# A hybrid decoder layer on one core: sums of weight blocks formed in the rounds of the FFNs and kept in HBM, and three orders changed

## Chip, core and metric

The kernel runs on 1 core of a Trainium2 chip, in one launch. The metric is the device time of that core in microseconds. Before the change it is 2225.57 us, the median of three runs (2220.57, 2225.57, 2229.49).

## What is computed

One layer on x of 1024 tokens x 1024 features, all in float32:

```python
h = swiglu(rmsnorm(x), w_gate, w_up, w_down)      # (silu(x@w_gate) * (x@w_up)) @ w_down, D_FF = 2816
x = x + 0.5 * rmsnorm(h)
h = hybrid_mixer(rmsnorm(x), ...)                 # one projection; dilated attention beside a Mamba-2 scan; w_out
x = x + rmsnorm(h)
h = swiglu(rmsnorm(x), ...)                       # second FFN, other weights
x = x + 0.5 * rmsnorm(h)
```

The change touches the two FFNs and the passage from the first FFN to the projection of queries, keys and values.

## The kernel before

**Split operands.** Every product of two float32 matrices is made of three matmuls on a high and a low part: w_hi x_hi, w_hi x_lo, w_lo x_hi. ScalarE rounds a raw tile to its high part (`*_hi`), VectorE subtracts (`*_lo`). TensorE can start when both are there.

**The FFN's rounds.** The 2816 inner features are 22 tiles of 128. The first two are computed plainly (`plain`, four units of a tile and half of the tokens: gate scaled, up scaled, SiLU on ScalarE, product, on VectorE L823 to L829). The other 20 run in pairs, i = 1 to 10 with s = 0, 1, each as seven block products of 12 matmuls (`seven_pe`) instead of eight: sums and differences of quarter blocks go in, and VectorE adds the results up (`tile` in `ffn_dve`). In the same tile VectorE forms the operands of the next one: L908 (t3, from the gate tile), L914 (t2), L919 (t1), L925 (t4, which needs the second up load), and the low parts L930 to L957. L957, the low part of the gate block, is the last. L1028 adds the gate product that must be read before product 7 of the tile overwrites its bank. L1012 and L1014 add the results of product 3; product 6 waits for L1014. i = 2 to 9 is a hardware loop on TensorE, ScalarE and VectorE; i = 10 (`LAST_PAIR`) is written out.

**SyncE** issues all loads and stores in the order of `ffn_sp`, and an instruction behind a waiting one waits too. In each tile (i, s): the gate load of the next tile (L413), once L957 has run; its first up load, once product 1 is done; the store of the tile before (L435); the second up load, once product 4 is done. Its loop is cut in two, i = 2 to 7 and i = 8 to 9. Between them `down_first_rows_sp` loads the first eleven activation tiles back from HBM (L1337, three transfers of 2048, 2048 and 1536 KB):

```python
rounds(2, FIRST_ROWS)            # FIRST_ROWS = 8
down_first_rows_sp(sp, p)
rounds(FIRST_ROWS, LAST_PAIR)
```

**The down phase** computes the activations times w_down, again as seven block products m = 0 to 6, each over eleven blocks k. A product's weights are one block of w_down or the sum or difference of two; of the seven, five are sums. Both blocks are loaded (`down_w_in`), VectorE adds them (`down_w_sum`, L1386), ScalarE makes the high part (L1401), VectorE the low part (L1417). Nine slots (eleven in the second FFN) hold blocks in flight. The first three blocks are prepared within the last tile.

**The planner.** From block 3 on, and through the turn to attention, the order on each engine is computed at build time: `Plan.order` simulates the engines with the costs and dependencies given in `add(engine, line, step, cost, *after)` and takes, at each moment, the step that can start first, by rank where several can. Only the order is used, not the times. `first_turn_steps` holds the turn: for each half h of the tokens and feature tile k, scale (L1605), residual (L1627), high (L1673) and low part (L1634) of the normed tile and its square. `first_group_steps` holds the first projection tiles: two query tiles preloaded, the key tile `w_in` 2 (L2444 high, L1977 low) and the weights of the values (`v_w_hi` L2326, `v_w_lo` L2291).

Of the kernel before, what the change touches and what calls it, by code (L numbers as in the profile page):

```python
# [81 lines left out]


def w_loads(p, m, k):
    n = down_slot_of(p, m, k)
    return sum(min(len(DOWN_W[a]), 2) for a in range(m + 1) for b in range(FG)
               if (a, b) <= (m, k) and down_slot_of(p, a, b) == n)


W_SUMS = FG * sum(len(u) > 1 for u in DOWN_W)  # L90
B_SUMS = FG * sum(len(u) > 1 for u in DOWN_B)
# [6 lines left out]
              "dn_b_lo": FG * DOWN_N, "dn_step": (FG - 1) * DOWN_N, "dn_mm": 4 * DOWN_N, "dn_put": len(PUTS),  # L98
              "dn_sum": len(SUMS), "dn_w_in9": 0, "dn_w_in10": 0}
for _n in range(9):  # L100
    FFN_COUNTS[f"dn_w_in{_n}"] = 16 * max(w_loads("f1", a, b) for a in range(DOWN_N) for b in range(FG)
                                          if down_slot_of("f1", a, b) == _n)
SHARED = {"dn_w_in0": ("turn_hi", KT), "dn_w_in1": ("turn_lo", KT), "dn_w_in2": ("turn_sq", KT), "dn_w_in3": ("turn_sum", KT - 1),
          "dn_w_in4": ("first_w_in", 16), "dn_w_in5": ("cols_in", 32), "dn_w_in6": ("consts_in", 64),
          "dn_w_in7": ("half_cols", 1), "dn_w_in8": ("first_w_hi", 1), "dn_b_first": ("first_w_lo", 1),
          "dn_b_second0": ("rope_sin", 2), "dn_w_in9": ("sd_x_mm", CH), "dn_w_in10": ("sd_cb_mm", CH)}
JOINT = {n: f"{old}_{new}" for new, (old, _) in SHARED.items() for n in (old, "ff_" + new)}


def build(nc, a):  # L110
    with ExitStack() as ctx:  # L111
        sems = {}

        def sem(name):
            if name[:3] in ("f1_", "f2_"):
                name = "ff_" + name[3:]
# [10 lines left out]
        def wait(eng, name, value):  # L127

            if not isinstance(value, int) or value > 0:

                eng.wait_ge(sem(name), value + (FFN_COUNTS[name[3:]] if name[:3] == "f2_" else 0)
                            + (SHARED[name[3:]][1] if name[3:] in SHARED and name[0] == "f" else 0))

# [127 lines left out]
        res3 = at("residual_closing", 0, [P, KT, S])  # L261
        late = at("late_tokens", 64, [P, KT, S])
        dw_hi, dw_two, dw_lo, dw_raw, db_hi, db_lo, db_raw = ({} for _ in range(7))
        for p, slots in DOWN_SLOTS.items():
# [13 lines left out]

        acts = nc.dram_tensor("act_scratch", (FT, P, S), F32).ap()
        x1 = nc.dram_tensor("x1_scratch", (KT, P, S), F32).ap()  # L280
        x2 = nc.dram_tensor("x2_scratch", (KT, P, S), F32).ap()
# [142 lines left out]
        def ffn_sp(sp, p, wgu):  # L424
# [21 lines left out]
            v_next(1, 1, 1)  # L446

            def rounds(first, last):
                with sp.Fori(first, last) as i:
                    g_next(i, 0)  # L450
                    v_next(i, 0, 0)
                    store(i - 1, 1)
                    v_next(i, 0, 1)
                    g_next(i, 1)
                    v_next(i, 1, 0)
                    store(i, 0)
                    v_next(i, 1, 1)
            rounds(2, FIRST_ROWS)
            down_first_rows_sp(sp, p)
# [194 lines left out]
        def ffn_act(act, p, t, pre):  # L654
# [79 lines left out]
            def tile(i, s, more):  # L734
# [9 lines left out]
                if is_first(i, s) and p == "f1":  # L744
                    plain(2)
                    plain(3)
                if s:
                    if more:
                        v_hi(i, s + 1, 0)
                    silu(e4, 0)  # L750
                    if not more:
                        for k in range(EARLY):
                            down_w_hi(act, p, 0, k)
                            down_b_hi(act, p, 0, k)
                    else:
                        t3_hi_act(i, s + 1)
                        t2_hi_act(i, s + 1)
                else:
                    v_hi(i, s + 1, 0)
                    t3_hi_act(i, s + 1)  # L760
                    t2_hi_act(i, s + 1)
                    silu(e4, 0)
                if more:
                    t1_hi_act(i, s + 1)
                    v_hi(i, s + 1, 1)
                    t4_hi_act(i, s + 1)
# [45 lines left out]
        def ffn_dve(v, p, t, pre):  # L812
# [50 lines left out]
            def first_round():  # L863
# [24 lines left out]
                s4_low(1)  # L888
                plain(2)
                plain(3)  # L890

# [109 lines left out]

            def tile(i, s, more):
                def product(n):
# [9 lines left out]
                had(1)  # L1013
                v.tensor_tensor(e4[:], banks(2), e2[:], ALU.add).then_inc(sem(p + "_read"), 1)  # L1014
                if not s:
                    t3_sum(i, s + 1)
# [12 lines left out]
                had(4)  # L1029
                v.tensor_tensor(e4[:], e4[:], rb[:, half(0)], ALU.mult).then_inc(sem(p + "_read"), 1)  # L1030
                if s and more:
                    t3_sum(i, s + 1)
# [31 lines left out]
                else:  # L1064
                    down_b_lo(v, p, 0, 2)
                    down_w_lo(v, p, 0, 2)
                wait(v, p + "_s_out", at_tile(i, s, 3, 3))
                v.tensor_tensor(stage[p][0][:, half(1)], u1[:], e2[:], ALU.mult)\
# [6 lines left out]
            with v.Fori(2, LAST_PAIR) as i:  # L1075
                tile(i, 0, True)
                tile(i, 1, True)
            tile(LAST_PAIR, 0, True)
# [14 lines left out]
        def down_steps(plan, p):  # L1093
# [8 lines left out]
            for m in range(DOWN_N):  # L1102
                for k in range(FG):
                    n = FG * m + k
                    ready = []
                    if n >= EARLY:
# [7 lines left out]
                        w = ("dw_in", m, k) if n >= slots else ("db_lo", m, k - 1) if k > EARLY else None  # L1114
                        if len(DOWN_W[m]) > 1:
                            add("DVE", "w_sum", ("dw_sum", m, k), 0.61, w)
# [167 lines left out]
        def w_sums(m, k):  # L1284
            return FG * sum(len(x) > 1 for x in DOWN_W[:m]) + k + 1

# [41 lines left out]
        def down_w_in(sp, p, m, k):  # L1328
            down_slot(sp, p, m, k)
            j = down_slot_of(p, m, k)  # L1330
            for n, (out, rows) in enumerate(DOWN_W[m][:2]):
                to = dw_two[p][j] if n else dw_raw[p][j]
# [19 lines left out]
        def down_start_sp(sp, p, store):  # L1352
            slots = len(DOWN_SLOTS[p])
            middle = slots - 4
            down_w_in(sp, p, 0, 0)
            down_w_in(sp, p, 0, 1)
# [38 lines left out]
        def down_w_hi(act, p, m, k):  # L1395
            j = down_slot_of(p, m, k)
            if len(DOWN_W[m]) > 1:
                wait(act, p + "_dn_w_sum", w_sums(m, k))
# [1918 lines left out]
```

## Time and profile before

| | us |
|---|---|
| median of three runs | 2225.57 |
| profiled execution, its own time | 2223.28 |
| span from its first to its last instruction | 2221.5 |
| TensorE busy | 2171.4 (98%) |
| VectorE busy | 1747.8 (79%) |
| ScalarE busy | 1012.4 (46%) |
| first FFN: rounds up to the down phase | 75 to 446 |
| second FFN: rounds up to the down phase | 1600 to 1993 |

PE is TensorE, DVE VectorE, ACT ScalarE, SP SyncE, POOL GpSimd. A bracket behind a row gives how long the engine was idle ahead of it and what it waited for. TensorE is nearly always busy, so the profile is read by its few gaps, and elsewhere by how close other engines come to making one.

### The profile page before, as it was taken

To read this page: it belongs to the slowest core of one execution; us is meant where nothing else is said; L and a number is where in the kernel's file an instruction comes from. 1 tells how busy PE (TensorE), PEld (TensorE's weight loads), DVE (VectorE), ACT (ScalarE), POOL (GpSimd) and SP (SyncE) were. 2 spreads that over 40 slices of the span, in tenths; PEclk is the share of its full clock that TensorE was granted. 3 is DMA by queue.
4 is the path that set the end of the run, shared out by engine and by line. 5 is a ranking of instruction groups with operands and counts; after the bars stand their busy time and mean duration, and the time that the engine had idled before them with its cause. 6 is when DMAs were issued, how large, how long until landed. Compare 5 with 4: busy or idle time off the path is not lost. (4 is left out here: it accounts for less than half of the span.)

```text
span 2221.5 us, 29464 instructions
## 1 busy us (share of the span) xinstructions
PE 2171.4 (98%) x10148; PEld 1776.9 (80%) x10148; DVE 1747.8 (79%) x2707; ACT 1012.4 (46%) x1837; POOL 229.3 (10%) x213
## 2 busy tenths in 40 slices
PE   9999999999999999999999999999999999999998
PEld 7788888878877777678788778788888888887887
DVE  8777777799898787786666686878877777779988
ACT  6333232255553576787632684314532333335454
POOL 0000000000000444444200233400000000000000
PEclk9999999999999999999999999999999999999999
DMA  4222243385453001001131134213232224247644
GB/s 146 69 83 84 85 136 137 106 306 180 162 192 99 28 10 39 31 18 58 40 105 48 57 114 161 95 50 137 80 95 85 82 83 169 88 150 278 222 141 159
DMA packets 101608, 245.00 MB, mean 110 GB/s; under 512 B 10752, under 2 KB 12800, under 8 KB 99968
## 3 DMA queue, kind: packets, MB, share of 16 engines
q1 hardware_dynamic: 101504, 243.65, 32.6%
q8 instruction: 60, 0.98, 0.2%
q14 instruction: 44, 0.36, 0.0%
HBM read 199.24 MB, written 44.37 MB: 110 GB/s over the span
## 5 line engine op out<-in xcount | busy, mean ns | idle before, releaser
L1428 PE MATMUL psum<-f_down_b_hi,f_down_w_hi 128*128 128x512 f32 x616 | 240.7, 391 | 6.2 <-DVE f_down_w_lo L1417 3.8
L1430 PE MATMUL psum<-f_down_b_hi,f_down_w_lo 128*128 128x512 f32 x616 | 239.7, 389 | 0.0
L1429 PE MATMUL psum<-f_down_b_lo,f_down_w_hi 128*128 128x512 f32 x616 | 239.7, 389 | 0.0
L711 ACT CAST plain_hi<-up_raw 128x512 fp32r<-128x512 f32 x78 | 48.3, 619 | 227.0 <-DMA up_raw<-in_gu 227.0
L737 ACT ACTIVATE sum<-sum 128x512 f32<-128x512 f32 x80 | 50.6, 633 | 209.5 <-DVE sum L1030 126.0
L1428 PEld LDWEIGHTS psum<-f_down_b_hi,f_down_w_hi 128*128 128x128 f32 x616 | 115.6, 188 | 33.7 <-DVE f_down_w_lo L1417 5.8
L715 ACT CAST t_hi<-t_raw 128x512 fp32r<-128x512 f32 x158 | 96.1, 621 | 95.2 <-DVE t_raw L925 81.6
L1430 PEld LDWEIGHTS psum<-f_down_b_hi,f_down_w_lo 128*128 128x128 f32 x616 | 115.7, 188 | 24.1
L1429 PEld LDWEIGHTS psum<-f_down_b_lo,f_down_w_hi 128*128 128x128 f32 x616 | 115.7, 188 | 23.8
L2241 PE MATMUL psum<-norm_hi,tile_hi 128*128 128x512 f32 x320 | 129.1, 403 | 1.8 <-DVE z_scaled L2663 1.8
L2570 DVE TENSOR_TENSOR probs_t_lo<-psum,probs_t_hi 128x512 fp32r<-128x512 f32 x144 | 97.2, 686 | 38.9 <-ACT probs_t_hi L2485 37.9
L472 PE MATMUL psum<-norm_hi,t_lo 128*128 128x512 f32 x320 | 125.1, 391 | 0.0
L2243 PE MATMUL psum<-norm_hi,tile_lo 128*128 128x512 f32 x320 | 124.9, 390 | 0.0
L2242 PE MATMUL psum<-norm_lo,tile_hi 128*128 128x512 f32 x320 | 124.8, 390 | 0.0
L472 PE MATMUL psum<-norm_hi,up_lo 128*128 128x512 f32 x320 | 124.5, 389 | 0.0
L470 PE MATMUL psum<-s_hi,t_hi 128*128 128x512 f32 x320 | 124.5, 389 | 0.0
L471 PE MATMUL psum<-s_lo,t_hi 128*128 128x512 f32 x320 | 124.5, 389 | 0.0
L472 PE MATMUL psum<-s_hi,t_lo 128*128 128x512 f32 x320 | 124.5, 389 | 0.0
L470 PE MATMUL psum<-norm_hi,t_hi 128*128 128x512 f32 x312 | 121.9, 391 | 2.5 <-DVE sum L1014 2.5
L1401 ACT CAST f_down_w_hi<-f_down_w_raw 128x512 fp32r<-128x512 f32 x154 | 95.0, 623 | 59.8 <-DVE f_down_w_raw L1386 59.7
L471 PE MATMUL psum<-norm_lo,t_hi 128*128 128x512 f32 x312 | 121.8, 391 | 0.0
L470 PE MATMUL psum<-norm_hi,plain_hi 128*128 128x512 f32 x312 | 121.5, 389 | 0.1
(406 smaller groups left out, 5812.7 us busy)
## 6 DMA issues: line engine op xcount, KB each, us to landing
f_down_w_raw<-in_d SPq DMA_DIRECT2D x154, 256.0 KB, 2.8
f_down_w_two<-in_d SPq DMA_DIRECT2D x110, 256.0 KB, 3.6
act_scratch<-act_stage_f SPq DMA_DIRECT2D x44, 512.0 KB, 5.3
gate_raw<-in_gu SPq DMA_DIRECT2D x40, 512.0 KB, 4.3
up_raw<-in_gu SPq DMA_DIRECT2D x80, 256.0 KB, 4.3
raw_tile<-in_w_att SPq DMA_DIRECT2D x28, 512.0 KB, 3.5
act_first_rows<-act_scratch SPq DMA_DIRECT2D x4, 2048.0 KB, 10.8
act_second_rows<-act_scratch SPq DMA_DIRECT2D x8, 1024.0 KB, 9.2
```

The lines of the kernel that those rows point to most:

```text
L470: pe.matmul(o, w_hi[:, k, :], a_hi(k), start=(k == 0 and not more), stop=False, skip_group_check=more)
L471: pe.matmul(o, w_hi[:, k, :], a_lo(k), start=False, stop=False, skip_group_check=more)
L472: mm = pe.matmul(o, w_lo[:, k, :], a_hi(k), start=False, stop=(k == KH - 1), skip_group_check=more)
L715: act.copy(to, of).then_inc(sem(p + "_t_hi"), 1)
L1401: act.copy(dw_hi[p][j][:], dw_raw[p][j][:]).then_inc(sem(p + "_dn_w_hi"), 1)
L1428: pe.matmul(o, dw_hi[p][j][:, d, :], db_hi[p][j][:], start=(k == 0), stop=False)
L1429: pe.matmul(o, dw_hi[p][j][:, d, :], db_lo[p][j][:], start=False, stop=False)
L1430: return pe.matmul(o, dw_lo[p][j][:, d, :], db_hi[p][j][:], start=False, stop=(k == FG - 1))
L2241: pe.matmul(banks(bank), wh[:, w % 2, k, :], nh[:, k, x], start=(k == 0), stop=False)
L2242: pe.matmul(banks(bank), wh[:, w % 2, k, :], nl[:, k, x], start=False, stop=False)
L2243: mm = pe.matmul(banks(bank), wl[:, w % 2, k, :], nh[:, k, x], start=False, stop=(k == KT - 1))
L2570: v.tensor_tensor(ptl[:, n % 2].rearrange("p a d -> p (a d)"), banks(4 + n % 2), pth[:, n % 2].rearrange("p a d -> p (a d)").bitcast(F32), ...
```

## The change

1. In the rounds i = 2 to 9, SyncE loads in each tile two blocks of w_down (256 KB each, `kept_in`), VectorE adds them (`kept_add`) between L953 and L1068 of the tile, and SyncE stores the sum to a tensor in HBM (`kept_store`). The tile (i, 0) forms block k = i + 1 of product 0, the tile (i, 1) that of product 6: 8 + 8 sums in each FFN. In the down phase these blocks are read by one load of the sum, and the steps `dw_sum` for them leave the plan. The buffers lie where the second plain tile was staged, so SyncE waits for its store before the rounds.
2. In the first tile of the first FFN, the last two units of `plain` move from ahead of the tile's sums to behind them: one behind L1014, one behind L1030; ScalarE's last SiLU accordingly.
3. In the plan of the turn, the key tile's load is given 7.0 instead of 4.0, its high part comes after the eighth normed tile's high part, and the values' low part after the eighth normed tile's low part.

```diff
+ROUND_SUMS = (0, DOWN_N - 1)
+ROUND_FIRST = 3
+ROUNDS = FG - ROUND_FIRST
+def kept_sum(m, k):
+    return m in ROUND_SUMS and k >= ROUND_FIRST
+def summed(m, k):
+    return len(DOWN_W[m]) > 1 and not kept_sum(m, k)
...
+            def kept_in(i, s):
+                wait(sp, p + "_kept_out", 16 * (2 * (i - 2) + s))
+                for n, (out, rows) in enumerate(DOWN_W[ROUND_SUMS[s]][:2]):
+                    w = a["d" + p[1]][FG * rows + ROUND_FIRST:FG * (rows + 1)]
+                    sp.dma_start((kept_two if n else kept_raw)[:], tile_of(w, i - 2)[:, 4 * out:4 * out + 4])\
+                      .then_inc(sem(p + "_kept_in"), 16)
+            def kept_store(i, s):
+                wait(sp, p + "_kept_sum", 2 * (i - 2) + s + 1)
+                sp.dma_start(tile_of(kept[ROUNDS * s:ROUNDS * s + ROUNDS], i - 2), kept_raw[:]).then_inc(sem(p + "_kept_out"), 16)
             def rounds(first, last):
                 with sp.Fori(first, last) as i:
                     g_next(i, 0)
                     v_next(i, 0, 0)
                     store(i - 1, 1)
                     v_next(i, 0, 1)
+                    kept_in(i, 0)
+                    kept_store(i, 0)
                     g_next(i, 1)
                     v_next(i, 1, 0)
                     store(i, 0)
                     v_next(i, 1, 1)
+                    kept_in(i, 1)
+                    kept_store(i, 1)
+            wait(sp, p + "_act_out", 16 * 2)
...
                 act.copy(e1[:], banks(first_bank(p, is_first(i, s)))).then_inc(sem(p + "_s_out"), 1)
                 if is_first(i, s) and p == "f1":
                     plain(2)
-                    plain(3)
...
                     silu(e4, 0)
+                    if is_first(i, s) and p == "f1":
+                        plain(3)
...
                 s4_low(1)
-                plain(2)
-                plain(3)
...
+            def kept_add(i, s):
+                wait(v, p + "_kept_in", 32 * (2 * (i - 2) + s + 1))
+                v.tensor_tensor(kept_raw[:], kept_raw[:], kept_two[:], DOWN_W[ROUND_SUMS[s]][2])\
+                 .then_inc(sem(p + "_kept_sum"), 1)
...
                 v.tensor_tensor(e4[:], banks(2), e2[:], ALU.add).then_inc(sem(p + "_read"), 1)
+                if is_first(i, s) and p == "f1":
+                    plain(2)
...
                 v.tensor_tensor(e4[:], e4[:], rb[:, half(0)], ALU.mult).then_inc(sem(p + "_read"), 1)
+                if is_first(i, s) and p == "f1":
+                    plain(3)
...
+                if keep:
+                    kept_add(i, s)
                 wait(v, p + "_s_out", at_tile(i, s, 3, 3))
...
-                        if len(DOWN_W[m]) > 1:
+                        if summed(m, k):
                             add("DVE", "w_sum", ("dw_sum", m, k), 0.61, w)
...
+            if kept_sum(m, k):
+                sp.dma_start(dw_raw[p][j][:], kept[ROUNDS * ROUND_SUMS.index(m) + k - ROUND_FIRST])\
+                  .then_inc(sem(f"{p}_dn_w_in{j}"), 16)
+                return
...
-            add("SP", "weights", ("w_in", 2), 4.0, downs)
+            add("SP", "weights", ("w_in", 2), 7.0, downs)
...
-            add("ACT", "weights", ("w_hi", 2), 1.05, ("w_in", 2), ("q_lo", 1))
+            add("ACT", "weights", ("w_hi", 2), 1.05, ("w_in", 2), ("q_lo", 1), ("hi", "t1", 0, KT - 1))
...
-            add("DVE", "v_w", ("v_w_lo",), 2.5, ("v_w_hi",))
+            add("DVE", "v_w", ("v_w_lo",), 2.5, ("v_w_hi",), ("lo", "t1", 0, KT - 1))
```

What is left out of the diff is the counting of semaphores, which the new steps share with others.

## Rows read from the trace of the kernel before

**Rows 1.** Page, part 1: busy time, share of the span, instructions.
```profile
PE 2171.4 (98%) x10148; PEld 1776.9 (80%) x10148; DVE 1747.8 (79%) x2707; ACT 1012.4 (46%) x1837; POOL 229.3 (10%) x213
```

**Rows 2.** TensorE's timeline, gaps: start, duration, engine, line, operation, [idle before, releaser].
```profile
75.66 0.47 PE L470 MATMUL psum<-norm_hi,t_hi 128*128 128x512 f32 x1 [2.47 <-DVE sum L1014]
...
347.86 0.50 PE L470 MATMUL psum<-s_hi_a,plain_hi 128*128 128x512 f32 x1 [0.88 <-DVE sum L1028]
...
455.83 0.50 PE L1428 MATMUL psum<-f_down_b_hi,f_down_w_hi 128*128 128x512 f32 x1 [0.66 <-DVE f_down_w_lo L1417]
...
670.74 0.55 PE L2262 MATMUL psum<-norm_hi,first_q_hi_lo 128*128 128x512 f32 x1 [2.52 <-DVE norm_lo L1634]
...
677.54 0.53 PE L2262 MATMUL psum<-norm_hi,first_q_hi_lo 128*128 128x512 f32 x1 [2.12 <-DVE norm_lo L1634]
...
2003.58 0.50 PE L1428 MATMUL psum<-f_down_b_hi,f_down_w_hi 128*128 128x512 f32 x1 [1.89 <-DVE f_down_w_lo L1417]
```

**Rows 3.** SyncE's timeline between rounds 7 and 8 of the first FFN.
```profile
324.15 1.50 SPq L1337 DMA_DIRECT2D act_first_rows<-act_scratch  x3
338.29 0.35 SPq L413 DMA_DIRECT2D gate_raw<-in_gu  x1
```

**Rows 4.** VectorE's timeline, end of tile (7,1) and tile (8,0).
```profile
335.82 0.68 DVE L953 TENSOR_TENSOR t_lo<-t_raw,t_hi 128x512 fp32r<-128x512 f32 x1
336.43 0.69 DVE L1068 TENSOR_TENSOR act_stage_f<-up,sum 128x512 f32<-128x512 f32 x1
...
343.86 0.69 DVE L908 TENSOR_TENSOR t_raw<-gate_raw 128x512 f32<-128x512 f32 x1 [3.39 <-DMA gate_raw<-in_gu]
...
347.12 0.68 DVE L1028 TENSOR_TENSOR sum<-psum,sum 128x512 f32<-128x512 f32 x1
```

**Rows 5.** View of the tile act_first_rows: landing of its six loads.
```profile
DMA to landing us min/median/max: 8.1/13.1/16.5
```

**Rows 6.** Page, parts 3 and 6: the queue, and a small load behind large ones.
```profile
q1 hardware_dynamic: 101504, 243.65, 32.6%
...
ident<-in_squares SPq DMA_DIRECT2D x1, 64.0 KB, 10.2
```

**Rows 7.** Timelines of SyncE, VectorE, TensorE, the same place of the second FFN.
```profile
1871.53 1.49 SPq L1337 DMA_DIRECT2D act_first_rows<-act_scratch  x3
...
1883.30 0.68 DVE L953 TENSOR_TENSOR t_lo<-t_raw,t_hi 128x512 fp32r<-128x512 f32 x1
...
1894.40 0.50 PE L470 MATMUL psum<-s_hi_a,plain_hi 128*128 128x512 f32 x1
```

**Rows 8.** Stretches: length, busy time (count) by engine, granted clock, DMA share, GB/s.
```profile
120.00:180.00 60.00, 60.00 (x267) 49.66 (x266) 43.66 (x69) 17.38 (x31) 0.00 (x0) 1.00 0.26 79
76.00:82.00 6.00, 6.00 (x21) 4.49 (x20) 5.63 (x10) 2.94 (x5) 0.00 (x0) 0.72 0.51 154
670.00:682.00 12.00, 9.13 (x30) 7.04 (x31) 11.69 (x15) 4.54 (x7) 0.00 (x0) 0.72 0.48 144
```

**Rows 9.** Timelines of VectorE and TensorE, one ordinary round of each FFN.
```profile
211.08 0.69 DVE L1028 TENSOR_TENSOR sum<-psum,sum 128x512 f32<-128x512 f32 x1 [2.12 <-PE psum L472]
...
231.64 0.68 DVE L1028 TENSOR_TENSOR sum<-psum,sum 128x512 f32<-128x512 f32 x1
...
232.56 0.39 PE L470 MATMUL psum<-s_hi_a,plain_hi 128*128 128x512 f32 x1
...
1740.65 0.68 DVE L1028 TENSOR_TENSOR sum<-psum,sum 128x512 f32<-128x512 f32 x1
...
1741.94 0.39 PE L470 MATMUL psum<-s_hi_a,plain_hi 128*128 128x512 f32 x1
```

**Rows 10.** SyncE's timeline, stores of the plain tiles.
```profile
74.22 0.82 SPq L441 DMA_DIRECT2D act_scratch<-act_stage_f  x2
```

**Rows 11.** Timelines of ScalarE and VectorE, turn to attention.
```profile
668.14 1.04 ACT L2444 CAST tile_hi<-raw_tile 128x1024 fp32r<-128x1024 f32 x1 [5.23 <-DMA raw_tile<-in_w_att]
...
674.30 2.42 DVE L2291 TENSOR_TENSOR v_weights_lo<-v_weights_raw,v_weights_hi 128x2176 fp32r<-128x2176 f32 x1
```

More of the change, by code:

```diff
@@ L81, in down_slot_of @@
     return (FG * m + k) % len(DOWN_SLOTS[p])
+ROUND_SUMS = (0, DOWN_N - 1)
[5 more added lines that the diff above has]
+    return len(DOWN_W[m]) > 1 and not kept_sum(m, k)
 def w_loads(p, m, k):
     n = down_slot_of(p, m, k)
-    return sum(min(len(DOWN_W[a]), 2) for a in range(m + 1) for b in range(FG)
+    return sum(2 if summed(a, b) else 1 for a in range(m + 1) for b in range(FG)
                if (a, b) <= (m, k) and down_slot_of(p, a, b) == n)
-W_SUMS = FG * sum(len(u) > 1 for u in DOWN_W)
+W_SUMS = sum(summed(a, b) for a in range(DOWN_N) for b in range(FG))
 B_SUMS = FG * sum(len(u) > 1 for u in DOWN_B)
@@ L99 @@
               "dn_sum": len(SUMS), "dn_w_in9": 0, "dn_w_in10": 0}
+KEPT = {"dn_w_in0": ("kept_in", 16 * 4 * ROUNDS), "dn_w_sum": ("kept_sum", 2 * ROUNDS),
+        "dn_b_second0": ("kept_out", 16 * 2 * ROUNDS)}
 for _n in range(9):
@@ L106 @@
           "dn_b_second0": ("rope_sin", 2), "dn_w_in9": ("sd_x_mm", CH), "dn_w_in10": ("sd_cb_mm", CH)}
+KEPT_OF = {kept: (new, count) for new, (kept, count) in KEPT.items()}
+for _n, (_, _count) in KEPT.items():
+    FFN_COUNTS[_n] += _count
 JOINT = {n: f"{old}_{new}" for new, (old, _) in SHARED.items() for n in (old, "ff_" + new)}
@@ L115, in sem @@
             if name[:3] in ("f1_", "f2_"):
-                name = "ff_" + name[3:]
+                name = "ff_" + KEPT_OF.get(name[3:], (name[3:],))[0]
             name = JOINT.get(name, name)
@@ L129, in wait, with offset @@
             if not isinstance(value, int) or value > 0:
-                eng.wait_ge(sem(name), value + (FFN_COUNTS[name[3:]] if name[:3] == "f2_" else 0)
-                            + (SHARED[name[3:]][1] if name[3:] in SHARED and name[0] == "f" else 0))
+                eng.wait_ge(sem(name), value + offset(name))
+        def offset(name):
+            p, rest = name[:3], name[3:]
+            if p not in ("f1_", "f2_"):
+                return 0
+            after = KEPT[rest][1] if rest in KEPT else 0
+            rest = KEPT_OF.get(rest, (rest,))[0]
+            return after + (FFN_COUNTS[rest] if p == "f2_" else 0) + (SHARED[rest][1] if rest in SHARED else 0)
         nh = at("norm_hi", 0, [P, KT, S], FR)
@@ L262, in build @@
         late = at("late_tokens", 64, [P, KT, S])
+        kept_raw = at("kept_weights", 160, [P, 4, P])
+        kept_two = at("kept_weights_two", 162, [P, 4, P])
         dw_hi, dw_two, dw_lo, dw_raw, db_hi, db_lo, db_raw = ({} for _ in range(7))
@@ L279, in build @@
         acts = nc.dram_tensor("act_scratch", (FT, P, S), F32).ap()
+        kept = nc.dram_tensor("kept_weight_sums", (len(ROUND_SUMS) * ROUNDS, P, 4, P), F32).ap()
         x1 = nc.dram_tensor("x1_scratch", (KT, P, S), F32).ap()
@@ L1000, in ffn_dve, with tile @@
                         turn_half_dve(v, step, e, cols[:, 24:32], cols[:, pre:pre + KT])
-            def tile(i, s, more):
+            def kept_add(i, s):
+                wait(v, p + "_kept_in", 32 * (2 * (i - 2) + s + 1))
+                v.tensor_tensor(kept_raw[:], kept_raw[:], kept_two[:], DOWN_W[ROUND_SUMS[s]][2])\
+                 .then_inc(sem(p + "_kept_sum"), 1)
+            def tile(i, s, more, keep=False):
                 def product(n):
@@ L1075, in ffn_dve @@
             with v.Fori(2, LAST_PAIR) as i:
-                tile(i, 0, True)
-                tile(i, 1, True)
+                tile(i, 0, True, True)
+                tile(i, 1, True, True)
             tile(LAST_PAIR, 0, True)
@@ L1284, in w_sums @@
         def w_sums(m, k):
-            return FG * sum(len(x) > 1 for x in DOWN_W[:m]) + k + 1
+            return sum(summed(x, y) for x in range(m + 1) for y in range(FG) if (x, y) <= (m, k))
         def b_sums(m, k):
@@ L1354, in down_start_sp @@
             middle = slots - 4
+            wait(sp, p + "_kept_out", 16 * 2 * ROUNDS)
             down_w_in(sp, p, 0, 0)
@@ L1396, in down_w_hi @@
             j = down_slot_of(p, m, k)
-            if len(DOWN_W[m]) > 1:
+            if summed(m, k):
                 wait(act, p + "_dn_w_sum", w_sums(m, k))
```

## The prediction

> **What bounds the kernel now.** I read the busy times first: TensorE is busy 98% of the span [rows 1], so a change can take away at most the 50 us in which TensorE stands still, and whatever makes it wait is added to the time one for one. So next I read TensorE's timeline for its idle places [rows 2]. Six of them matter here: 2.47 us in the first tile of the first FFN, 0.88 us in its round 8, 0.66 and 1.89 us at block k=3 of the two down phases, and 2.52 and 2.12 us in the turn to attention. Elsewhere in the rounds TensorE has no gap, so what counts there is how late VectorE, SyncE and the transfers may be before one opens. For that I read VectorE's and SyncE's timelines around one gate load [rows 3, 4, 7, 9] and how transfers land [rows 5, 6]. Last, the granted clock after gaps [rows 8]. Matmuls are shown 0.39 us long but start every 60/267 = 0.225 us [rows 8]; a gap therefore costs about 0.16 us more than the idle time shown.
>
> **Rounds, part 1: the first-rows loads change place.** This is the largest term. In each round SyncE gets, behind the last up load of a tile, two loads (256 KB each) and one store of 256 KB. That store waits until VectorE has added the pair. VectorE does this add in the same tile after L953. SyncE executes in order, so everything behind the store waits as well. Behind the last round of the first loop (tile (7,1)) stand the three act_first_rows loads, 2 + 2 + 1.5 MB, and behind these the gate load of round 8.
>
> Before, the first-rows loads were issued at 324.15, right behind the last up load of the tile, and the gate load at 338.29, 14.1 us later [rows 3]. Afterwards: the added operation takes the place at 336.43 of the one that now follows L953 [rows 4], and ends at 337.1; store issued at 337.3, the first-rows loads at 337.7: 13.5 us later than before. The gate load is then issued behind them, at about 339.3.
>
> Does the gate load have to wait for 5.6 MB? Three loads are issued within 1 us, and over both phases they landed 8.1 (least), 13.1 (median) and 16.5 us (most) after issue [rows 5]: one after the other and not together. A 64 KB constant issued behind the x tiles took 10.2 us, and all but 0.1 MB for instructions is on one queue, q1 [rows 6]. So transfers are served in the order of issue. Before, the last first-rows piece landed at about 325 + 16.5 = 341.5 and the gate data at 343.8, already late: VectorE waited 3.39 us for it, and TensorE 0.88 [rows 4, 2]. Afterwards both move by the 13.5 us: gate data at 357.3, the chain from L908 to L1028 takes 347.12 - 343.86 = 3.26 us as before [rows 4], so L1028 starts at 360.6 and, 0.74 later as before (347.12 to 347.86 [rows 4, 2]), product 7 of tile (8,0) at 361.3 instead of 347.86. That is +13.5 us. In the second FFN: first rows 1871.53, L953 at 1883.30, so the added operation ends at 1884.6 and the first rows go out at 1885.2, +13.7 us; so product 7, at 1894.40 before, is 13.7 us later [rows 7]. Sum +27.2. Bounds: if the gate load were served beside the first rows with a share of 1/4, 0.5 MB would take some 5 us and not 1.3, so about +4 each; upper end 14.5 each if the new 256 KB also moves ahead of them (1.5 MB, the last piece, landed 3.4 us behind the one before it [rows 5], which makes 0.6 us for 256 KB).
>
> The Trainium skill ("DMA: Bandwidth & Descriptors", Queues, rings and completion order) says that an engine takes descriptors of one ring in order, but alternates between queue rows packet by packet. By its second half the gate load would pass between the first rows, and the sum would be that of rival A; the trace shows one queue for all of it, so I go by the first half.
>
> After a stop of that length the clock will be down. After the 2.47 us gap the granted clock averaged 0.72 over 6 us, after the two gaps of the turn 0.72 over 12 us [rows 8]. 0.28 x 6 = 1.7 us; two stops, +3.4 (0 to 7).
>
> **Rounds, part 2: every other round.** VectorE runs without a pause from L1028 of tile (i,1), which still waited 2.12 us for TensorE [rows 9], to the gate's low part; SyncE issues the next gate load on that; L1028 of the next tile must end before product 7. Slack there: L1028 starts at 231.64, needs the 0.74 us, product 7 starts at 232.56: 0.2 us. In the second FFN 1740.65 and 1741.94: 0.55 us [rows 9]. The added operation (0.61 us) stands in this stretch, so the gate load leaves 0.61 us later and product 7 is late by 0.4 and 0.06 to 0.2 us. Seven rounds a phase (the eighth is counted above): 7 x 0.45 + 7 x 0.15 = +4.2. The add in tile (i,0) is absorbed by the 2.12 us. Bounds 0 and +13: the latter if the store of 256 KB also delays each gate load by its 0.6 us of transfer; it is issued 1.9 us before, so mostly gone.
>
> **Down phases.** Of 11 blocks in products 0 and 6, k = 3 to 10 lose their sum and one of two loads: 32 VectorE operations of 0.69 us and 32 loads less in all. They lie beside TensorE work except at block k=3 of product 0, where TensorE waited 0.66 and 1.89 us for the weights' low part, each with the 0.16 us [rows 2]: 2.9 us. Without the sum the high part can be formed as soon as the load lands and goes ahead of the b parts in the planned order. I take -2.5 (-2.9 to +1: the load itself may be late). The tail, after product 6, is counted at 0 (-2 to +1): 8 sums less stand before it, but TensorE there waited for the rows' scale, not for weights.
>
> **Turn to attention.** ScalarE waited 5.23 us for tile 2 with norm_hi queued behind, so norm_lo came late and TensorE stood 2.52 us; then v_weights_lo (2.42 us) ran ahead of the last norm_lo, 2.12 us more [rows 11, 2]. Both now come behind the eighth norm part. Lost there: 4.64 us, twice 0.16, and 0.28 x 11 = 3.1 of clock [rows 8], 8.0 in all. What is late next: VectorE needs scale, residual, low and square sum for each part, one every 0.61 us [rows 4] or a little more, so 2.5 us a part against 6 matmuls, 1.36 us, of TensorE; then tile 2's low part. Some 2 us of smaller waits stay, without a loss of clock. -6 (-8 to 0).
>
> **First tile.** The two plain products (6 operations, 4.1 us with their waits for ScalarE) leave the place ahead of the tile's sums. Before, product 6 waited for L1014, the second sum, and began at 75.66, where 73.03 was possible [rows 2]: 2.6 us lost, and 1.7 of clock [rows 8]. Now L1014 ends near 71.4, and product 6 isn't late. But the first plain product (2.1 us) still stands before L1028, which then ends near 77.5 where product 7 could start at 75.75: 1.8 us. The last plain product ends 6 us later, at 80.3 instead of 74.2. SyncE waits for it with the two stores and the up load behind them (at 74.22 before [rows 10]), so the up data lands near 85.5, 5 us behind it; VectorE waits in L925, two operations later L939's result is there at 87.0, and product 3 of the next tile (three products of 2.72 us behind product 7's 77.55, 85.7) is 1.3 us late. 4.3 lost before, 1.8 + 1.3 = 3.1 after: -1.2 (-2.6 to +3).
>
> **Sum.** +27.2 + 3.4 + 4.2 - 2.5 - 6 - 1.2 = +25.1 us. The profiled execution took 2223.3 us (span 2221.5), 2.3 below the median of the three, 2225.6, which ran from 2220.6 to 2229.5. I predict 2249 us.
>
> **Rivals.**
> A, on the other side: the gate load isn't held by the first rows (served beside them or ahead). For it: before, the gate load landed only 5.5 us after its issue with first rows still moving. Against it: the ordered landings [rows 5]. Point of decision: gate data under 5 us after issue. Then +27.2 and 3.4 fall away, -5.5: 2218 us, chance 0.09. The variant in which the rounds cost nothing either and all gains reach their ends (-8, -2.9, -2.6, -1) gives 2209, chance 0.04.
> B: the new 256 KB store delays each gate load by its transfer, and the stall grows to 1.1 and 0.8 us a round: +9 more, 2258 us. For it, the slack is only 0.2 us [rows 9]; against it, the store's data should have moved before the gate's. Chance 0.10.
> C: fair sharing among the queued transfers, +4 for each phase and little loss of clock: 27.2 + 3.4 become 8 to 10, about 2227. For it nothing in the landings. Chance 0.03.
> The forecast: 0.74.
>
> **How the numbers follow.** One can tell 0.5%, 11 us, from no change. The forecast and B are slower: 0.84, with 0.01 for C's upper end, 0.85. A and C's rest give 0.11 no change, and 0.04 is faster. The forecast's own bounds run from 2235 (turn and down at their best, clock free) to 2260; the range reaches to 2234 and to B's 2260.
>
> **What would show it.** Right: the act_first_rows loads issued 13 to 14 us later, straight ahead of a gate load; that load landing 17 us or more after issue; VectorE at L908 waiting about 17 us for gate_raw, TensorE idle some 13 us before a product 7, once in each FFN; granted clock 0.5 behind it; gaps of 0.1 to 0.6 us before product 7 in the other rounds; no gap at block k=3; 670 to 678 nearly closed. Wrong: act_first_rows landing spread over the same time as the gate load, or a gate load landing in under 6 us behind them.

## The result

The changed kernel takes 2248.38 us (median of 4, 2244.3 to 2256.15) against 2225.23 us (median of 4, 2220.57 to 2229.49), 23.2 us more: slower by about 1%, ratio 1.0113 with a 95% interval of 1.0094 to 1.0131. All ratios here leave out one execution, of e_turn, that took 2705 us at a granted clock of 0.75. The forecast was 2249 us, range 2234 to 2260, slower with 0.85. The profiled execution spans 2246.2 us against 2221.5, +24.7; the forecast's sum was +25.1. Its largest term, the two stops, was right. That the whole sum came so close was luck: several terms that were not right cancelled. They are taken apart below.

### The profile after

TensorE's busy time has not grown (2169.5 us against 2171.4), so all of the 24.7 us is standing still. Page, part 1 (against [rows 1]):

```profile
PE 2169.5 (97%) x10148; PEld 1773.1 (79%) x10148; DVE 1749.3 (78%) x2707; ACT 1012.6 (45%) x1837; POOL 229.7 (10%) x213
```

TensorE's timeline, its gaps in the FFNs (against [rows 2]; lines have moved, L514 is the old L470, L1078 the old L1028):

```profile
78.06 0.47 PE L514 MATMUL psum<-s_hi_a,plain_hi 128*128 128x512 f32 x1 [1.71 <-DVE sum L1078]
88.50 0.50 PE L514 MATMUL psum<-s_hi,t_hi 128*128 128x512 f32 x1 [2.03 <-DVE t_lo L987]
92.17 0.47 PE L514 MATMUL psum<-norm_hi,plain_hi 128*128 128x512 f32 x1 [0.66 <-ACT first_product L787]
...
273.79 0.50 PE L514 MATMUL psum<-s_hi_a,plain_hi 128*128 128x512 f32 x1 [0.29 <-DVE sum L1078]
...
365.04 0.80 PE L514 MATMUL psum<-s_hi_a,plain_hi 128*128 128x512 f32 x1 [14.37 <-DVE sum L1078]
...
1827.40 0.50 PE L514 MATMUL psum<-s_hi_a,plain_hi 128*128 128x512 f32 x1 [1.08 <-DVE sum L1078]
...
1919.39 0.79 PE L514 MATMUL psum<-s_hi_a,plain_hi 128*128 128x512 f32 x1 [14.80 <-DVE sum L1078]
```

The two large ones are what the forecast put first. Neither they nor the smaller ones name a transfer: the releaser is VectorE, and one has to go on to VectorE's timeline to see what it waited for. There (against [rows 4]) the added sum L1047 stands at the end of tile (7,1), and the first operation of the next operands waits 16.87 us for the gate data:

```profile
340.12 0.69 DVE L1047 TENSOR_TENSOR kept_weights<-kept_weights,kept_weights_two 128x512 f32<-128x512 f32 x1
...
361.04 0.69 DVE L951 TENSOR_TENSOR t_raw<-gate_raw 128x512 f32<-128x512 f32 x1 [16.87 <-DMA gate_raw<-in_gu]
...
364.30 0.68 DVE L1078 TENSOR_TENSOR sum<-psum,sum 128x512 f32<-128x512 f32 x1
```

SyncE's timeline says why (against [rows 3]): the store of the sum, the first-rows loads right behind it, then the gate load.

```profile
340.97 0.35 SPq L485 DMA_DIRECT2D kept_weight_sums<-kept_weights  x1
341.58 1.57 SPq L1395 DMA_DIRECT2D act_first_rows<-act_scratch  x3
343.50 1.19 SPq L441 DMA_DIRECT2D gate_raw<-in_gu  x1
```

Before, there were 14.1 us between the first rows and the gate load; now 1.9. The view of act_first_rows has the same landings as [rows 5] to 0.1 us, so those loads are not slower:

```profile
DMA to landing us min/median/max: 8.0/13.1/16.6
```

The view of gate_raw between 335 and 375 has one load, and it is slower:

```profile
DMA to landing us min/median/max: 17.4/17.4/17.4
```

The granted clock is at its lower level (0.50 of 2.4 GHz) in the stop and for some microseconds after work begins again. The first two rows are the stretches behind the two stops, the third is the first stop itself (columns as in [rows 8]):

```profile
366.00:372.00 6.00, 6.00 (x19) 4.71 (x18) 5.61 (x10) 2.11 (x5) 0.00 (x0) 0.64 0.00 0
1920.00:1924.00 4.00, 4.00 (x12) 3.13 (x11) 3.72 (x7) 2.21 (x4) 0.00 (x0) 0.57 0.00 0
354.00:366.00 12.00, 0.96 (x2) 0.84 (x3) 4.86 (x8) 1.92 (x4) 0.00 (x0) 0.50 0.80 299
```

TensorE does the same 10148 matmuls in both kernels, all but a few in the turn and at the end in the same order. So its lag, by how much a given matmul starts later than in the kernel before, gives the account by stages. In the two profiled executions the lag grew by:

| stage | forecast | measured |
|---|---|---|
| start to product 7 of tile (1,1) | -1.2 | +1.2 (0.4 of it ahead of the first tile) |
| rounds without round 8, first / second FFN | +3.1 / +1.1 | +3.5 / +3.9 |
| product 7 of tile (8,0), first / second FFN | +13.5 / +13.7 | +13.5 / +14.8 |
| the tile behind it (clock) | +1.7 / +1.7 | +2.5 / +1.9 |
| start of the down phase, first / second FFN | -2.5 together | -1.3 / -2.2 |
| turn to attention | -6 | -8.3 |
| attention to the second FFN's first tile | 0 | -3.8 |
| after product 6 of the second FFN | 0 | -0.9 |

### The profile page after: what moved, and what is told of

The parts are those of the page before. It is cut to its first block, busy times and chain, and to the rows that moved or that the text cites. A ratio compares the mean times of both kernels' runs of the same rounds, so it can differ in the third digit from the quotient of the medians.

```text
span 2246.2 us, 29800 instructions
## 1 busy us (share of the span) xinstructions
PE 2169.5 (97%) x10148; PEld 1773.1 (79%) x10148; DVE 1749.3 (78%) x2707; ACT 1012.6 (45%) x1837; POOL 229.7 (10%) x213
## 4 chain that ended last, share of the span: by engine, by line
PE 71%; DVE 14%; DMA 5%; issue 4%; ACT 3%; POOL 1%; SPq 0%; DVEq 0%; ACTq 0%; POOLq 0%
PE psum L514 7%; PE psum L515 7%; PE psum L516 7%; PE psum L1487 6%; PE psum L1489 6%; PE psum L1488 6%; PE psum L2300 3%; PE psum L2302 3%; PE psum L2301 3%; DMA gate_raw<-in_gu 2%; PE psum L2454 2%; DMA up_raw<-in_gu 2%; PE psum L651 2%; PE psum L653 1%; PE psum L652 1%
## 5 line engine op out<-in xcount | busy, mean ns | idle before, releaser
L514 PE MATMUL psum<-s_hi,t_hi 128*128 128x512 f32 x320 | 124.6, 389 | 2.0 <-DVE t_lo L987 2.0
L1471 ACT CAST f_down_b_hi<-f_down_b_raw 128x512 fp32r<-128x512 f32 x110 | 68.6, 626 | 120.1 <-DVE f_down_b_raw L1451 120.1
L514 PE MATMUL psum<-norm_hi,plain_hi 128*128 128x512 f32 x312 | 121.6, 390 | 0.7 <-ACT first_product L787 0.7
L514 PE MATMUL psum<-norm_hi,t_hi 128*128 128x512 f32 x312 | 121.4, 389 | 0.0
```

Source lines behind the costliest of these rows:

```text
L514: pe.matmul(o, w_hi[:, k, :], a_hi(k), start=(k == 0 and not more), stop=False, skip_group_check=more)
L1471: act.copy(db_hi[p][j][:], of).then_inc(sem(p + "_dn_b_hi"), 1)
```

## The experiments

### The first rows, both ways

**a_rows_back**: the changed kernel with round 7 written out for SyncE, and in it

```diff
                 kept_in(i, 1)
+                if rows:
+                    down_first_rows_sp(sp, p)
                 kept_store(i, 1)
```

> The changed kernel, but the three first-rows loads are issued between the last round's pair of block loads and its store of the sum, so they don't wait for VectorE's added operation. Theory (the first rows were moved in front of a gate load that then waits for 5.6 MB): both long stops before product 7 of tile (8,0), 14.4 and 14.8 us of idle time, fall to 1 to 3 us (the first rows leave about 1 us later than in the kernel before, behind 512 KB of new loads), and no loss of clock: 30 us less than the changed kernel's 2248, 2216 to 2220 us, 0.3% faster than the kernel before. Rival (the added work of the rounds as a whole, VectorE's sums and 50 MB/s more traffic, makes the stops): the stops stay above 8 us, 2240 or more.

Measured: 2223.93 us, ratio to the kernel before 1.0001 (0.9992 to 1.0011). TensorE's gaps at the two places:

```profile
353.42 0.79 PE L519 MATMUL psum<-s_hi_a,plain_hi 128*128 128x512 f32 x1 [2.62 <-DVE sum L1083]
...
1897.32 0.50 PE L519 MATMUL psum<-s_hi_a,plain_hi 128*128 128x512 f32 x1 [1.91 <-DVE sum L1083]
```

The place of two lines makes 24.4 us. That is less than the 30 I expected, and the theory's 2216 to 2220 was missed. What stays of the two stops costs 5.2 us of lag with the clock, where the theory had idle times of 1 to 3 us and no loss of clock. And the changed kernel's profile had been lucky elsewhere: between attention and the second FFN its lag shrank by 4.2 us, while that of a_rows_back grew by 1.3 (below). The rival (stops above 8 us) is out; its traffic, 121 to 126 GB/s in the rounds against 83 to 85 before by part 2 of the pages, is some 40 GB/s more, not 50 MB/s.

**b_rows_late**: the kernel before, nothing of the change, one wait:

```diff
             rounds(2, FIRST_ROWS)
+            wait(sp, p + "_t_lo", at_tile(FIRST_ROWS, 0, 7, 6))
             down_first_rows_sp(sp, p)
```

> The kernel before with one wait more: SyncE issues the first-rows loads only when VectorE has run L953 of tile (7,1), in each FFN. No block sum, no other change. Theory: the gate load stands behind them and lands 13 us later, TensorE stops about 13.5 us before product 7 of tile (8,0) and pays 2 us of clock, twice: +29 to +32 us, 2253 to 2257 us. Rival (the order alone is harmless, the transfers share the engines): below 2235 us.

Measured: 2255.83 us, ratio 1.0132 (1.0113 to 1.0152), as expected. Gaps of TensorE and, between them, VectorE's wait in the first FFN:

```profile
359.78 0.80 PE L471 MATMUL psum<-s_hi_a,plain_hi 128*128 128x512 f32 x1 [12.56 <-DVE sum L1029]
...
1923.11 0.80 PE L471 MATMUL psum<-s_hi_a,plain_hi 128*128 128x512 f32 x1 [12.08 <-DVE sum L1029]
```

```profile
355.79 0.69 DVE L909 TENSOR_TENSOR t_raw<-gate_raw 128x512 f32<-128x512 f32 x1 [15.07 <-DMA gate_raw<-in_gu]
```

So the place of these three loads alone is enough for a slowdown of the size of the whole change, and the block sums are not needed for it.

**g_gate_first**: the changed kernel with round 8 written out:

```diff
                 g_next(i, 0)
+                if rows:
+                    down_first_rows_sp(sp, p)
                 v_next(i, 0, 0)
```

> The changed kernel, but the gate load of round 8 is issued ahead of the first-rows loads; its first up load still stands behind them. Theory (transfers land in the order of issue, whatever they are for): the gate data lands in 4 to 5 us and VectorE no longer waits for it, but then waits some 15 us for up_raw at the next operation, and both stops stay at 13 to 15 us: 2245 to 2250 us. Rival (the stop has to do with the gate load's own size or place, or with the tile's work): both stops under 5 us, 2220 to 2226 us.

Measured: 2252.66 us, ratio 1.0125 (1.0103 to 1.0147), 2.7 us above the range, with TensorE's stops at 14.45 and 13.98 us as the theory had them. VectorE's timeline:

```profile
348.30 0.69 DVE L956 TENSOR_TENSOR t_raw<-gate_raw 128x512 f32<-128x512 f32 x1 [2.76 <-DMA gate_raw<-in_gu]
363.23 0.69 DVE L962 TENSOR_TENSOR t_raw<-t_raw,up_raw 128x512 f32<-128x512 f32 x1 [14.24 <-DMA up_raw<-in_gu]
```

The gate data, issued ahead at 343.4, is there 4.9 us later; the up load, half its size and issued behind, takes the stop over. It is the order of issue that decides, not which load it is. The Trainium skill ("DMA: Bandwidth & Descriptors", Queues, rings and completion order) says that on each DMA engine descriptors are consumed in ring order, and the waits of 2.76 and 14.24 us agree with it. Rival A's passing of the first rows was not seen in any run: in all twelve profiles and both FFNs the first gate or up load issued behind them landed 0.6 to 3.0 us behind their last piece.

### The turn and the first tile, each alone

**e_turn**: the kernel before with part 3 of the change.

> The kernel before with the three edits of the turn to attention alone (key tile's load given 7.0, its high part behind the eighth high part, the values' low part behind the eighth low part). Theory: the two gaps at 670 and 677 close and the clock stays up: -7 us there, as between the traces of before and after (12.3 us of offset instead of 19.4), 2216 to 2220 us. Rival (the eight sums of product 6 that are gone from VectorE's list gave the room, not the order): -3 us or less, 2221 to 2226, with VectorE still late for the norm parts.

Measured: 2220.03 us, ratio 0.997 (0.996 to 0.9981), a little faster, clear of the noise. The two gaps of [rows 2] are replaced by smaller ones, and the clock stays up:

```profile
671.09 0.47 PE L2262 MATMUL psum<-norm_hi,first_q_hi_lo 128*128 128x512 f32 x1 [0.34 <-DVE norm_lo L1634]
673.82 0.47 PE L2262 MATMUL psum<-norm_hi,first_q_hi_lo 128*128 128x512 f32 x1 [1.09 <-DVE norm_lo L1634]
676.66 0.40 PE L2367 MATMUL psum<-v_weights_hi,norm_hi 128*128 128x272 f32 x1 [1.22 <-DVE v_weights_lo L2291]
```

From the first gap behind L1563's result in product 6 to the first score of attention it takes 108.2 us, before 113.6, in the changed kernel 105.3. So the edits give 5.4 us. The remaining 2.9 come with the block sums: the six profiles with them and the edits gain 8.3 to 8.4 us here, the three with the edits alone 5.4 to 5.5. All three gaps above wait for VectorE, which without the block sums has eight sums more in product 6; whether the eight loads that also fall away have a part was not tried. Theory and rival each hold a part.

Of the 5.4 us some 2.5 are clock, and not certain. b_rows_late has the turn of the kernel before, with gaps of 1.57, 0.92 and 2.64 us, and there the clock did not fall, where in the kernel before and in f_first_tile it fell twice. It took 2.5 us less for the turn than the kernel before. Its stretch at the turn (columns as in [rows 8]):

```profile
684.00:698.00 14.00, 9.78 (x55) 8.19 (x56) 11.81 (x16) 4.92 (x9) 0.00 (x0) 1.00 0.51 152
```

**f_first_tile**: the kernel before with part 2 of the change.

> The kernel before with the moved plain products of the first tile alone. Theory: it gains nothing, since the stores and the up load behind the last plain product leave 6 us later: gaps of 1.7, 2.0 and 0.7 us for the one of 2.5 with its loss of clock, +0.5 us at product 7 of tile (1,1), 2224 to 2228 us, no change that can be measured. Rival (the forecast's -1.2, the gaps of the changed kernel come from its start): 2222 to 2225 with the offset at tile (1,1) below zero.

Measured: 2228.16 us, ratio 1.0012 (1.0000 to 1.0025), in the profile +1.8 us at tile (1,1), of which 0.3 stood there before the first tile. It loses a little, more than I expected, and the clock fell behind the second gap. In the changed kernel's timelines of VectorE and SyncE one sees the cause; part of it I had left out of the prediction:

```profile
85.12 0.69 DVE L1097 TENSOR_TENSOR act_stage_f<-first_product,sum 128x512 f32<-128x512 f32 x1 [2.62 <-DMA act_scratch<-act_stage_f]
86.95 0.69 DVE L968 TENSOR_TENSOR t_raw<-up_raw,t_raw 128x512 f32<-128x512 f32 x1 [1.14 <-DMA up_raw<-in_gu]
```

```profile
80.73 0.82 SPq L469 DMA_DIRECT2D act_scratch<-act_stage_f  x2
```

The stores of the plain tiles leave at 80.73 instead of 74.22. VectorE waits first for them (the tile's result goes where the first plain tile lies) and then for the up load behind them.

### Towards a better version

**c_turn_rows**: the kernel before, part 3 of the change, and the first rows behind the second up load of tile (8,0):

```diff
                 v_next(i, 0, 1)
+                if rows:                 # i = 8
+                    down_first_rows_sp(sp, p)
                 g_next(i, 1)
```

> The kernel before with the three edits of the turn, and with the first-rows loads moved half a tile later: behind the second up load of tile (8,0), so that the next gate load is that of an s = 1 tile, which VectorE wants 8.8 us after its issue and not 4.4. No block sum in the rounds, no change of the first tile. Theory (it is the gate load behind the first rows that stops TensorE, and only where it is wanted at once): no gap before product 7 of any tile of round 8, 1 to 1.6 us less in the first FFN and up to 1.6 in the second, and -7.4 of the turn as measured: 2215 to 2218 us. Rival (5.6 MB in flight disturb whichever tile they meet): a gap of over 1 us somewhere in tiles (8,0) to (9,0), 2219 or more.

Measured: 2218.81 us, ratio 0.9972 (0.9959 to 0.9985). No gap in round 8 of either FFN; TensorE's lead grows by 1.0 us in the first and 0.3 in the second. The median is 0.8 us outside what I expected, and one step of the expectation was wrong: -7.4 us was e_turn's whole lead at the start of the second FFN, not what the turn had been measured at. The turn gave 5.4 us here as there; the rest lay in a stretch of unchanged code where this profile lost 2.0 us, with five falls of the clock between 1340 and 1600.

**d_kept_last**: c_turn_rows plus the block sums, added behind the gate's low part, stored behind the gate load (first and last round apart):

```diff
                 g_next(i, 0)
+                kept_store(i - 1, 1)
                 v_next(i, 0, 0)
...
                 g_next(i, 1)
+                kept_store(i, 0)
                 v_next(i, 1, 0)
```

> c_turn_rows plus the 16 block sums, but off the gate's chain: VectorE adds behind the gate's low part, and SyncE stores the sum behind the next gate load. Theory (the sums cost in the rounds only because they delay the gate load by 0.6 us): the gaps of 0.2 to 1.2 us before product 7 go, the gains at the start of the down phases stay (1.3 and 2.2 us in the changed kernel's trace): 3.5 us less than c_turn_rows, 2212 to 2215. Rival (the traffic of the added loads and stores delays the gate data too): gaps stay, no better than c_turn_rows.

Measured: 2217.68 us, ratio 0.9968 (0.9958 to 0.9979), no better than c_turn_rows, as the rival had it. The gains were there, but the gaps before product 7 stayed; TensorE and VectorE:

```profile
195.47 0.50 PE L522 MATMUL psum<-s_hi_a,plain_hi 128*128 128x512 f32 x1 [0.85 <-DVE sum L1085]
```

```profile
229.57 0.69 DVE L960 TENSOR_TENSOR t_raw<-gate_raw 128x512 f32<-128x512 f32 x1 [2.24 <-DMA gate_raw<-in_gu]
230.82 0.69 DVE L966 TENSOR_TENSOR t_raw<-t_raw,up_raw 128x512 f32<-128x512 f32 x1 [0.56 <-DMA up_raw<-in_gu]
```

My theory of this run was too narrow: freeing the gate load was not enough, since the store now stood ahead of the up load, which L966 needs at once. k_store_last tests this.

**k_store_last**: the same with the store one step later:

```diff
                 g_next(i, 0)
-                kept_store(i - 1, 1)
                 v_next(i, 0, 0)
                 store(i - 1, 1)
+                kept_store(i - 1, 1)
...
```

> d_kept_last with the store of each sum moved once more: behind the first up load and the store of the activations, not between the gate load and the up load. In d_kept_last the gaps before product 7 stayed at 0.3 to 0.85 us, and VectorE waited 0.5 to 0.7 us for up_raw behind the gate data. Theory (what is left of the rounds' cost is the up load, which left 0.4 us later and behind 256 KB): the gaps close, the first FFN's rounds cost under 1 us and not 5, the gains of the down phases and of the turn (7 us together) stay: 2211 to 2214 us, 3 to 4 less than d_kept_last. Rival (the two added loads or VectorE's sum by itself make the gaps): the rounds still cost 4 us, 2216 to 2219.

Measured: 2210.57 us, ratio 0.9949 (0.9936 to 0.9963), 0.4 us under the range; the kernel before ran at 2223.09 beside it, against 2225.55 beside d_kept_last, so the ratios and not the medians are to be compared: 0.2% less. From tile (1,1) to tile (7,1) of the first FFN TensorE's lag grows by 0.1 us, where it grew by 4.0 in d_kept_last. VectorE does as many sums and as many bytes move, so neither of these made d_kept_last's gaps; the place of the store did. One new gap of 1.6 us in each FFN is left, behind the first rows:

```profile
370.58 0.49 PE L522 MATMUL psum<-norm_hi,plain_hi 128*128 128x512 f32 x1 [1.55 <-DVE up_lo L982]
```

**h_first_tile2**: c_turn_rows, with the first plain tile stored early, `plain(2)` at the end of tile (1,0), `plain(3)` behind L1014 of tile (1,1), and the second plain tile stored behind tile (1,0)'s store:

```diff
+            if p == "f1":
+                wait(sp, p + "_prod", 2)
+                plain_store(0)
             g_next(1, 0)
...
             v_next(1, 1, 1)
+            if p == "f1":
+                wait(sp, p + "_act_out", 16 * 2)
+                wait(sp, p + "_prod", 4)
+                plain_store(1)
```

> c_turn_rows plus another cure of the first tile: its last two plain products go to the end of tile (1,0) and behind L1014 of tile (1,1), where VectorE idled 2.6 and 3.3 us; the first plain tile is stored early, the second behind the store of tile (1,0), so that no load stands behind them. Theory (the moved products cost their gain only by the stores and the up load that waited for them): no gap in the first tile, -2.6 us and the clock's 1.7 where it fell: 4 us less than c_turn_rows at product 7 of tile (1,1), 2211 to 2214 us. Rival (VectorE has no 4 us to spare in these tiles): a new gap of 1 us or more in tile (1,1) or (2,0), no better than c_turn_rows.

Measured: 2215.59 us, ratio 0.9949 (0.9931 to 0.9968), 1.6 us above the range. One gap stays in the first tile, 1.07 us, where I had expected none. It was there in c_turn_rows too, behind the one of 2.46 us:

```profile
79.45 0.47 PE L475 MATMUL psum<-s_hi_a,plain_hi 128*128 128x512 f32 x1 [1.04 <-DVE sum L1033]
```

From 70 us to tile (1,1) TensorE gains 3.1 us on the kernel before, in c_turn_rows 0.4. The difference of 2.7 is the gap of 2.46 us that is closed and the 0.16 of its price; the expected 4 counted clock as well, and c_turn_rows's profile had lost none there.

**j_all**: k_store_last and h_first_tile2 together.

> All that paid, together: k_store_last plus h_first_tile2's first tile. Theory (the parts touch different places, so they add): h_first_tile2's 2215.6 less the 7 us of the block sums at the down phases, the turn and the end, 2208 to 2211 us, 0.7% faster than the kernel before and the fastest of all. Rival (the parts share one slack of VectorE in tiles (1,0) to (2,1)): a gap of over 1 us there and no better than k_store_last.

Measured: 2208.78 us (2206.89 to 2210.07), ratio 0.9937 (0.9923 to 0.9951), as expected. It is the fastest version that ran, 0.6% (14 us) under the kernel before, which took 2223.09 beside it, and some 40 us under the changed one, with all parts of the change in it and only their places different. Against k_store_last the median is 1.8 us less, with intervals that overlap; between the two profiles the first tile gave 2.6 us.

## Why the forecast was right, step by step

The mechanism, place and size of the largest term were right, and the experiments show it. The other terms were off by 1 to 4 us each, one of them in its sign, and it is luck that their errors cancelled.

**The first rows** (+27.2): right in mechanism, place and size. Measured 13.5 and 14.8 us; a_rows_back and b_rows_late show it from both sides, g_gate_first the rule behind it. The first-rows loads went out 17.4 us later than before (341.58 against 324.15), 3.7 of it the lag of the rounds and 13.7 the delay that the forecast put at 13.5; 17.4 us to landing is one load standing behind three. One reading beside it was wrong: parts 3 of the pages have 0.98 and 0.36 MB of instructions on two other queues, not 0.1 MB; against the 243.65 MB of q1 this changes nothing. The price of a gap, its idle time and 0.16 us, held: where the 2.47 us gap at 75 closed, TensorE came 2.62 us earlier.

**The clock after the stops** (+3.4): 2.5 and 1.9, so 4.4. The row after a 2.5 us gap was too mild a model for a stop of 14 us: the clock stood at 0.50 when work began again, while in [rows 8] part of the stretch ran at the full one.

**The other rounds** (+4.2): 7.4. The first FFN came out as worked out (3.5 against 3.1). In the second the step that failed is "slack 0.55 us against 0.61": between 1775 and 1865 the five gate loads took 4.4 to 5.0 us to land, where the same five had taken 4.0 to 4.5 (VectorE waited up to 3.1 us for one), and single rounds lost 0.4, 0.6 and 1.2 us. This profile alone does not fix the split: a_rows_back and g_gate_first have the same rounds, and theirs lost 4.4 and 4.6 us in the first FFN and 1.7 and 2.5 in the second, 6.1 and 7.1 in all. So the term was 2 to 3 us too small whichever profile is taken. d_kept_last and k_store_last show which resource it was in d_kept_last: every load of the operands that are formed first must be free of what was added, the up load too. In the changed kernel the sum stands ahead of the gate load as well, and which part of the 7.4 is the sum's time and which the store's transfer was not separated. Rival B had the right thought, the transfer of the store, but not its size in the changed kernel.

**Down phases** (-2.5): -3.5, beyond their best bound of -2.9. Both gaps at block k=3 are gone. The tail, counted at 0, gave 0.9 us; all six profiles with the block sums have 0.9 to 1.0 there, the others nothing.

**Turn** (-6): -8.3. The 2 us of smaller waits that I kept were those of e_turn, 3.1 us with the price of each gap; the block sums removed them. I counted the eight sums of product 6 only at the tail of the second FFN and not in the turn behind the first, where they gave 2.9. The clock that I counted as lost before, 3.1 us (by [rows 8] 0.28 x 12 = 3.4), was worth 2.5 by b_rows_late, and only where it fell.

**First tile** (-1.2): the wrong sign. The tile itself cost 0.8 us in the changed kernel, in a_rows_back and in g_gate_first, and 1.4 in f_first_tile, where the clock fell; the rest of +1.2 and +1.8 stood there at 70 us. Two steps failed. One is "VectorE waits in L925" as the only wait behind the late stores; the wait of L1097 for the stores themselves was missed. The other is the 1.7 us of clock counted as lost before. In c_turn_rows the same gap brought no fall, and TensorE then waited 1.04 us for VectorE before product 7 instead (row above), so without the fall it was only 0.4 us faster here. Slower matmuls had filled a wait that was coming anyway.

**Not foreseen** (-3.8): between attention and the second FFN, where the code is the same. This is chance. Before, four short stretches ran at a lower clock; after, only one of the same four places did (kernel before, then after):

```profile
1354.00:1362.00 8.00, 5.56 (x18) 4.22 (x17) 2.82 (x4) 2.10 (x2) 0.00 (x0) 0.79 0.66 228
1394.00:1400.00 6.00, 6.00 (x23) 4.85 (x23) 2.48 (x5) 3.89 (x5) 6.00 (x4) 0.72 0.54 186
1548.00:1556.00 8.00, 7.66 (x38) 6.34 (x38) 7.97 (x15) 3.99 (x7) 0.00 (x0) 0.79 0.26 98
1578.00:1584.00 6.00, 6.00 (x30) 5.04 (x29) 6.00 (x10) 2.49 (x4) 0.00 (x0) 0.72 0.23 87
```

```profile
1366.00:1374.00 8.00, 5.53 (x25) 4.37 (x24) 3.90 (x5) 2.37 (x3) 0.00 (x0) 1.00 0.67 242
1400.00:1408.00 8.00, 7.72 (x42) 6.66 (x43) 7.28 (x9) 3.67 (x4) 7.09 (x4) 1.00 0.86 306
1556.00:1564.00 8.00, 7.65 (x48) 6.46 (x46) 7.97 (x15) 3.96 (x8) 0.00 (x0) 1.00 0.23 86
1584.00:1590.00 6.00, 6.00 (x29) 5.04 (x28) 6.00 (x10) 3.31 (x6) 0.00 (x0) 0.72 0.29 111
```

0.21 of 8 or 0.28 of 6 us, 1.7 us each, are lost or not. In c_turn_rows's profile there are five such stretches, in e_turn's one. Behind a gap of 1 to 2.5 us or a run of one-column matmuls (as at 1575 in the kernel before) it varied between executions whether the clock fell. The lag follows the clock: the changed kernel's profile has one of the highest clocks of the twelve over the stage, and from 1340 on its lag shrank by 4.2 us; b_rows_late's has the lowest, and its lag grew by 4.1 (changed kernel, then b_rows_late):

```profile
1340.00:1615.00 275.00, 270.54 (x1289) 223.01 (x1288) 222.77 (x287) 111.31 (x149) 41.77 (x16) 0.99 0.30 106
1340.00:1615.00 275.00, 269.96 (x1249) 221.76 (x1250) 216.22 (x278) 104.84 (x140) 40.88 (x16) 0.96 0.29 102
```

The terms that I had too low (first tile, first rows, clock and rounds, 7.7 us by the table) and those too high (down, turn, tail and this one, 8.0) nearly cancelled. That is why +25.1 met +24.7; the mechanism accounts for the two stops, and that the rest came to nearly nothing is chance.

Open: why single gate loads of the second FFN take up to 0.8 us longer beside the stores was not tried by itself.

## What to carry to other kernels

A store that waits for a computation, put into an in-order issue queue, moves everything behind it to that computation's time. Look in particular at what stands behind the *last* turn of a loop, not only at the loop's steady state. Bulk loads belong behind the loads that are wanted soonest and ahead of those with slack: here the same work cost 23 us or gained 14 us by its place among the same instructions. When an operation is moved, list who waits for the stores that its result allows, as well as who waits for the result.

## What was new about the hardware

In these runs a load issued behind several large ones on the same queue waited for them: in all 24 places the first gate or up load behind the three first-rows loads landed 0.6 to 3.0 us behind their last piece, and 0.5 MB behind 5.6 MB took 17.4 us against 4.4 alone. The order is not strict for loads close together. In the kernel before, raw_tile, issued at 661.45, took 6.7 us to land, and a load of cos, issued at 661.88, took 4.4, so it landed 1.9 us ahead of it; the largest such lead in the twelve profiles is 2.3 us.

After gaps of 1 to 2.5 us the clock's fall was not repeatable: the gap of about 2.5 us in the first tile brought it down in three profiles of six (kernel before, b_rows_late and e_turn; 0.72 over 6 us) and not in the others (c_turn_rows, d_kept_last and k_store_last). This makes differences of 2 to 8 us between single profiles over stages of the same code. And a fall costs less than its share of the stretch where TensorE would have had to wait behind it: 0.4 us instead of 1.7 in the first tile.
